# Two layers on one core: where a turn and the splits of the merged rows stand

## The reference

```
h = rmsnorm(x)
s_c  = q . k_cmp * scale + bias                 # 31 compressed blocks of keys, per head
p_c  = softmax(s_c) where a block is visible
o_c  = p_c @ v_cmp
o_s  = attention over the selected blocks (16 of 8: all of them)
o_w  = attention over a window of 512
o_nsa  = gate0 * o_c + gate1 * o_s + gate2 * o_w
x = x + (g_nsa * o_nsa + g_conv * o_conv + g_mem * o_mem) @ w_out
x = x + 0.5 * ffn(rmsnorm(x))
```

## Time and profile before

| what | value |
|---|---|
| median of 3 runs | 2500.01 us |
| the runs | 2498.63, 2500.01, 3254.33 us |
| the profiled execution's own time | 2499.84 us |
| its span (first to last instruction) | 2498.0 us |
| mean granted clock of TensorE | 0.992 of full |
| TensorE busy | 2435.6 us (98% of the span) |
| VectorE busy | 1410.5 us (56%) |
| ScalarE busy | 969.4 us (39%) |
| GpSimd busy | 176.6 us (7%) |

### The profile page before, as it was taken

One profiled execution on the slowest core, in us unless ns is written; L12 is line 12 of the kernel. 1 busy time (PEld: TensorE's weight loads), 2 busy tenths in 40 slices (PEclk: granted clock), 3 DMA queues, 4 the chain that ended last, 5 costly groups with the idle time before them and its releaser, 6 DMA issues.

```text
span 2498.0 us, 31231 instructions
## 1 busy us (share of the span) xinstructions
PE 2435.6 (98%) x11978; PEld 2032.0 (81%) x11978; DVE 1410.5 (56%) x2919; ACT 969.4 (39%) x1798; POOL 176.6 (7%) x244
## 2 busy tenths in 40 slices
PE   9999999999999999889999999999999998999997
PEld 7888888888887878778888888878878887888886
DVE  6435445676667666765443445667644566643444
ACT  4223234432345545653322334555423345422321
POOL 0000000101002211320000000222200002000000
PEclk9999999999999999999999999999999999999998
DMA  4454434333321122003223224211122432223222
GB/s 151 109 130 133 104 116 135 102 102 111 108 84 52 60 68 74 29 26 118 94 88 106 101 85 138 77 51 60 51 69 93 134 118 68 93 88 106 93 92 86
DMA packets 86381, 231.36 MB, mean 93 GB/s; under 512 B 8488, under 2 KB 23464, under 8 KB 86234
## 3 DMA queue, kind: packets, MB, share of 16 engines
q1 hardware_dynamic: 78768, 217.22, 26.8%
q10 hardware_dynamic: 7466, 12.14, 2.5%
HBM read 217.79 MB, written 11.53 MB: 92 GB/s over the span
## 4 chain that ended last, share of the span: by engine, by line
PE 91%; DVE 5%; ACT 3%; issue 1%; ACTq 0%; DMA 0%; POOL 0%; SPq 0%; DVEq 0%
PE bank L955 89%; PE bank L1148 2%; DVE t_PS L1843 0%; ACT t_PS L1441 0%; ACT t_pp L1580 0%; ACTq L1517 0%; DVE t_wlo L1838 0%; DVE t_pp L2072 0%; DVE t_QS L2165 0%; ACT t_whi L1441 0%; ACT t_tmp L1441 0%; PE bank L1322 0%; DMA t_XT<-in_xT 0%; DVE t_ST L2339 0%; DVE t_XT L2417 0%
## 5 line engine op out<-in xcount | busy, mean ns | idle before, releaser
L955 PE MATMUL bank<-t_XH,t_whi 128*128 128x512 f32 x2064 | 813.3, 394 | 5.9 <-DVE t_sa L2072 4.0
L955 PE MATMUL bank<-t_XH,t_wlo 128*128 128x512 f32 x2064 | 804.3, 390 | 0.0
L955 PE MATMUL bank<-t_XL,t_whi 128*128 128x512 f32 x2064 | 803.8, 389 | 0.0
L1838 DVE TENSOR_TENSOR t_wlo<-t_raw,t_whi 128x1024 fp32r<-128x1024 f32 (+2 forms) x418 | 479.5, 1149 | 373.7 <-ACT t_whi L1441 370.6
L1441 ACT ACTIVATE t_whi<-t_raw 128x1024 fp32r<-128x1024 f32 (+3 forms) x422 | 415.6, 988 | 418.9 <-PE bank L955 362.5
L955 PEld LDWEIGHTS bank<-t_XH,t_whi 128*128 128x128 f32 x2064 | 387.8, 188 | 89.6 <-DVE t_sa L2072 5.5
L955 PEld LDWEIGHTS bank<-t_XH,t_wlo 128*128 128x128 f32 x2064 | 387.5, 188 | 82.2
L955 PEld LDWEIGHTS bank<-t_XL,t_whi 128*128 128x128 f32 x2064 | 388.0, 188 | 77.3
L955 PE MATMUL bank<-t_RX,t_whi 128*128 128x512 f32 x1056 | 325.1, 389 | 0.0
L1942 DVE TENSOR_TENSOR t_tmp<-bank,t_RB 128x512 f32<-128x512 f32 x178 | 122.5, 688 | 227.2 <-PE bank L955 222.2
L955 PEld LDWEIGHTS bank<-t_RX,t_whi 128*128 128x128 f32 x1056 | 198.2, 188 | 41.2
(11 more groups left out here) (313 smaller groups left out, 2748.6 us busy)
## 6 DMA issues: line engine op xcount, KB each, us to landing
t_raw<-in_f_in SPq DMA_DIRECT2D x86, 512.0 KB, 3.2
t_raw<-in_f_out SPq DMA_DIRECT2D x32, 384.0 KB, 3.1
t_raw<-in_w_conv SPq DMA_DIRECT2D x24, 512.0 KB, 3.2
t_raw<-in_w_merge SPq DMA_DIRECT2D x24, 512.0 KB, 3.2
t_raw<-in_fg SPq DMA_DIRECT2D x22, 512.0 KB, 3.2
t_raw<-in_fu SPq DMA_DIRECT2D x22, 512.0 KB, 3.2
t_raw<-in_f_out SPq DMA_DIRECT2D x32, 320.0 KB, 2.8
t_raw<-in_w_g SPq DMA_DIRECT2D x16, 512.0 KB, 3.2
```

The lines of the kernel that those rows point to most:

```text
L955: return e.matmul(o, l, r, start=start, stop=stop, skip_group_check=True)
L1838: e.tensor_tensor(wlo[n % NRAW][:, 0:width], raw[n % NRAW][:, 0:width], f32(whi[n % NHI][:, 0:width]), ALU.subtract).then_inc(*w_lo.tick(n))
```

## The change

There are two edits.

1. `cturn(g)` is tied to tile 3 of head `(2, 1)` instead of tile 1. That is two steps of `attend` later, in each of the four groups. It then stands in the same step as the gate unit and the values that read its result, in front of them.
2. `attend` gets an argument `ending`, a list of items to be put into the steps behind the last score, from the second such step on, one in each step, behind the rest copy. The sparse stage gives it `msplit` for blocks 0 to 5. `project_out` then starts with block 6 for `pj` 0. For `pj` 1 it starts with 7 (6 + 1) as before.

```diff
--- before.py
+++ after.py
@@ -338,7 +338,7 @@
         w.add("widefin", what, h)
         yield 18
 
-    def attend(heads, jobs, total=0, lag=5, vlag=3):
+    def attend(heads, jobs, total=0, lag=5, vlag=3, ending=()):
 
 
         base = len(w.tiles)
@@ -392,6 +392,8 @@
                 unscaled.append(base + t)
             if lag <= t < n + lag:
                 w.add("rest", base + t - lag)
+            if n < t <= n + len(ending):
+                ending[t - n - 1]()
             w.catch_up(1)
             if t >= lag + vlag:
                 hd, i = w.tiles[base + t - lag - vlag]
@@ -538,7 +540,7 @@
             small = {(1, 0): {0: one("cclear", g), 2: one("cscore", g), 3: one("cback", g)},
                      (1, 1): {0: one("csoft", g, 0), 1: one("csoft", g, 1), 2: one("csoft", g, 2), 3: one("csoft", g, 3)},
                      (2, 0): {0: one("cnorm", g, 0), 1: one("cnorm", g, 1), 2: one("cnorm", g, 2), 3: one("cnorm", g, 3)},
-                     (2, 1): {1: one("cturn", g)}}
+                     (2, 1): {3: one("cturn", g)}}
             for r in range(4):
                 for a in range(2):
                     p, q = r // 2, 2 * (r % 2) + a
@@ -565,13 +567,13 @@
                         more = dict(before=before, after=after)
                     heads.append(Head("spa", 0, range(4), g=g, r=r, a=a, p=p, q=q, at=at, **more))
         left = 4 * KD - sum(item[0] in ("conv", "convg") for item, _ in w.items)
-        attend(heads, jobs, 24 * left + 4 * 60 + 8 * 24 + 26 + 72)
+        attend(heads, jobs, 24 * left + 4 * 60 + 8 * 24 + 26 + 72, ending=[one("msplit", 0, k) for k in range(6)])
         while w.able(jobs):
             w.step(jobs)
 
     def project_out(name, pj, nxt, jobs):
         w.add("banks", OPEN)
-        for k in range(7 * pj, KD):
+        for k in range(6 + pj, KD):
             w.add("msplit", pj, k)
         for m in range(KD):
             w.lin("po", pj, m, name=name, j=m)
```

## The result

| what | before | after |
|---|---|---|
| median of 20 runs each | 2499.99 us | 2494.61 us |
| ratio of the two, with its 95% interval | | 0.9978 [0.9971, 0.9984] |
| profiled execution's span | 2498.0 us | 2492.6 us |
| mean granted clock in the profile | 0.992 | 0.992 |

The change makes the kernel 5.4 us faster; the interval of the ratio is 4.0 to 7.2 us. One execution before (3254 us) and two after (2723 and 5482 us) lie far outside the rest and do not move the medians. The forecast was 2494.4, so the sum is hit within 0.2 us. Whether its terms are, only the traces and the experiments can say.

A forecast was written before the change was run, and what follows sets the result against it. TensorE, 91% of the chain, was taken as the bound, so only its idle time and low-clock stretches count. From 2499.84, -4.1 (splits) and -1.5 (turns) give 2494.2, as a median 2494.4 us; own case 2492 to 2496, rival B and drift to 2501.

The forecast's parts named there:

- The tail, -4.1: End of sparse stage: with early splits the output projection reaches its second unit 4.1 us sooner, 2.4 gap and 1.7 clock.
- The 1.7 us for the clock: First projection unit: TensorE's low clock after the 2.2 us wait costs 1.7 us, all counted as saved.
- Group 0, +1.6: Group 0's gate unit: TensorE newly idles about 2 us for the convolution unit's bank, a loss of 1.6 us.
- The bank in dispute: Group 0: the gate unit takes the PSUM bank the convolution unit took six takes before, which VectorE evacuates late.
- Group 3, -1.4: Group 3's gate unit starts 1.4 us earlier, as VectorE's 1.6 us leaves the path of the next score's read.
- Groups 1 and 2, -0.7 and -1.0: The next long unit starts 0.7 us earlier in group 1 and 1.0 in group 2; no low-clock stretch counted as saved.
- The sum of the turns, -1.5: Moving the turn in all four groups: +1.6 - 0.7 - 1.0 - 1.4 = -1.5 us.
- P: The prediction's own sum: turns +1.6, -0.7, -1.0, -1.4 in groups 0 to 3, splits -4.1.
- A: Rival: turn waits 7.7, two low-clock stretches 3.4 and tail 4.1 all vanish, no group 0 loss; 15.2 us, 2484.8; 6%.
- B: Rival: gains of groups 1 to 3 vanish and group 0's clock falls, or tail gives 2.4 alone; 2497.5 mid; 29%.
- C: Rival, slower: TensorE waits for late values in every group's first four-head sum; +7.2 us, 2507; 6%.
- D: Rival: unit order shifts, or splits queue before the last copy; within 5 us either way; 5%.

The follow-up runs named there:

- the splits alone: Kernel before with only the six early splits, the turn staying at tile 1: 2496.08 us, ratio 0.9984.
- the turn alone: Kernel before with only the turn moved to tile 3 in all four groups, splits late; run twice: 2497.66 us (ratio 0.9988) and 2497.75 us (0.9991).
- the two experiments on the ring: The change with the turn's result in a sum's bank outside the ring: 2492.04 us; kernel before with one ring bank passed over in group 0: 2505.45 us.
- the series of medians: Against the kernel before: six early splits, 2496.08 us; with the turn also moved in group 3, 2494.13; in groups 1 to 3, 2493.23; whole change, 2494.61.
- the profile of group 3 alone: Kernel before with the turn moved to tile 3 in group 3 only, splits late: 2497.15 us, ratio 0.9987.

## Why the prediction was right, and where only its sum was

**The tail, -4.1.** The mechanism is right in each step: the start behind the last values, three splits on each side of the last copy, the weight split pushed back to 1115.85 at no cost, SyncE's six reads ahead of the gate's weight load. The medians of the splits alone give -4.0. The 1.7 us for the clock rested on one profile's low stretch, which is no fixed property of the wait. Of seven profiles with the wait of 2.2 for the first split, five have the lower level behind it and two full clock. Both of the two are of the kernel with the turn alone, and both profiles of the kernel before have the lower level; whether the turn's move or luck made the difference, the profiles don't show. For the kernel before no profile speaks against the 1.7. Against the Trainium skill (TensorE: Matmul & The Clock Gate, "Why this matters for your kernels"), which would call such a gap too short, five of seven profiles speak against the rule and two for it; by the rule's 2.4 the tail would be short of the measured 4.0, inside its interval.

**Group 0, +1.6.** Right in cause and size: +1.8. The wait in the profile is 1.44 where about 2 was forecast; the last 0.4 of the interval I can't place. The bank in dispute was named right, and the two experiments on the ring show it.

**Group 3, -1.4.** Right: -1.5, in every profile with the turn moved there. VectorE's copy of the turned rows, 1.6 us, leaves the path of the next score's read. Before, the copy (`t_PCT`) and the pieces of `VC` stand between the rest copy and the score's read (`t_pp`):

```profile
1089.52 0.69 DVE L1843 TENSOR_TENSOR t_PCT<-bank,t_PCT 128x512 fp32r<-128x512 f32 x1 [0.17 <-ACT t_PCT L1441]
1090.25 0.97 DVE L2252 TENSOR_TENSOR t_VC<-t_vcn,t_vch 32x64 fp32r<-32x64 f32 x4
1091.25 0.42 DVE L2072 CUSTOM_DVE_ANT_0 t_pp<-bank,t_TB 128x256 f32<-128x256 f32 x1
```

After, the read follows the rest copy at once, and `t_PCT` starts 2.5 us behind it:

```profile
1088.86 0.69 DVE L1845 TENSOR_TENSOR t_PS<-bank,t_PS 128x512 fp32r<-128x512 f32 x1 [0.32 <-ACT t_PS L1443]
1089.46 0.42 DVE L2074 CUSTOM_DVE_ANT_0 t_pp<-bank,t_TB 128x256 f32<-128x256 f32 x1
...
1091.91 0.69 DVE L1845 TENSOR_TENSOR t_PCT<-bank,t_PCT 128x512 fp32r<-128x512 f32 x1 [0.66 <-ACT t_PCT L1443]
```

The Trainium skill (Perfetto Trace Analysis, "Optimization Strategy") asks for the awaited work to come sooner or end sooner, by which moving the waiter would give 0. Here the waiter's own follow-up work had stood ahead of the next awaited read, so moving it did make that read sooner.

**Groups 1 and 2, -0.7 and -1.0.** Both mis-sized: +0.4 and -0.3 by the intervals, and nothing by the median of the kernel with these two alone. In group 1 the waits came where the forecast put them (892.38 and 894.64), and the unit starts 8.3 us behind the values that open the interval for a forecast 8.1. In group 2 the unit starts at 23.6 for a forecast 23.4, but the wait is another one: the forecast had the last score wait for the rest copy, and the score before it waits 4.14 for VectorE's read of a score. What was left out is behind the unit. The sum gave 0 for the clock at both places, "because about as much idle time stays ahead of each". In group 1 the idle time comes in two pieces now, and the lower level is granted for longer (0.57 against 0.79 over 893 to 901), which hands back about what the earlier start won. In group 2 the scores and turns run at the lower level, 0.6 to 1.2 us a piece, as the forecast assumed, but now the gate unit's first matmuls do too (0.63 a matmul, before 0.39). From the start of the unit to the values behind it, five profiles with the turn moved take 5.9 to 6.3 us, and six without 5.6 (a seventh, the one with 31.4 in the table, 7.0). So the step that failed is the clock put at nothing at these two places.

**The sum of the turns, -1.5.** The whole change against the splits alone is -1.4, and the series of medians (-4.0, -5.5, -7.0, and -5.4 with group 0) follows P's -4.1, -5.5, -7.2, -5.6. That agreement is partly luck, as each median has 2 us of doubt and two of the four terms are wrong by 0.7 to 1.1 us. The intervals of the whole change add up to +0.4 - 4.1 = -3.7, and 5.4 was measured. Something outside them makes up the 1.7; a clock that stands higher elsewhere is a candidate (0.91 against 1.00 over 370 to 390 in the two profiles), but it isn't shown. What also stays open is why the turn alone gives 2.3 to 3.0, where its profiles account for 1.2. That the turn and the splits together give less than both parts (5.4 of 6.6, a difference that the intervals cover) fits a stretch of low clock in the tail that either of them can avert, but the profile of group 3 alone does not show it averted.

**The rivals.** A (the waits go whole) needed 15 us and fails: the stall of 3.9 is 4.1 now, at a score. B said that the ring eats the turn's gain, and that is nearly what the intervals show (+0.4 in sum), in groups 0 to 2; only its other half, a tail of 2.4 or a low clock in group 0, is not in the profile after. C (late values) did not happen: no wait stands at the values of any group. D: the order of units is unchanged, and the splits stand where the edit puts them.

## What to carry to other kernels

A wait at an in-order engine's late input can be walked past, but first ask which buffer each of the overtaking takers wants: with a ring, moving one take by two places changes the partner of every taker between. Giving the moved item a buffer outside the ring took away group 0's loss here (17.65 us for the interval, not 19.2); by the medians it was worth 2.6 us (2494.6 to 2492.0, in separate comparisons whose intervals overlap). The gain that stays, in group 3, is the work behind the moved item leaving another engine's queue ahead of an awaited read, not the wait that disappears from the list. And when single us count, look at the mean granted clock of every run before reading two profiles against each other: one profile's low stretch is not yet a term of a sum. Nor is span x (1 - clock) the price of the clock; what 0.001 of it costs is read from many runs of one kernel.

## What was not expected of the hardware

- The same wait of 2.20 us, for the first split, was followed by the lower clock level in five profiles and by full clock in two (both of the kernel with the turn alone). A wait of 2.4 in the sparse stage (L1148 for a score's read) had full clock around it in the profile before (1.00 over 770 to 789) and 0.91 in the profile after. What decides, the rows don't say.
- Over 97 runs of one program 0.001 of mean granted clock goes with about 1.3 us of time ((2502.7 - 2497.5) / 4), half of what 0.001 of 2500 us is. A straight line in the clock takes away half of the standard deviation between its runs (1.9 to 0.9 us).
- Six reads of 256 KB issued in a row took SyncE 5.41 us, 0.90 each, where eight took 4.53, 0.57 each, because they now follow the splits as these come, one by one.
